# A two-layer diffusion trunk on one core: in the second mixer, VectorE gates the convolved x tile before the next weight split instead of after it

## What is computed

```
def ssd_mixer(h, hc, w_in, conv_w, conv_b, dt_bias, a_log, d_skip, gn_w, w_out):
    ...
    def project(t):
        z, xbc, dt = jnp.split(t @ w_in, [SSD_D_INNER, 2 * SSD_D_INNER + 2 * G * N], axis=-1)
        xbc = jax.nn.silu(conv_centred(xbc, conv_w, conv_b)).astype(jnp.float32)
        xs, Bm, Cm = jnp.split(xbc, [SSD_D_INNER, SSD_D_INNER + G * N], axis=-1)
    ...
    for d, rev in ((0, False), (1, True)):
        yc_d, hc_d = ssd_chunk_scan(f(xc), f(dtc[:, :, d]), A[d], f(Bc), f(Cc), h0)
        yl_d, _ = ssd_chunk_scan(f(xl), f(dtl[:, :, d]), A[d], f(Bl), f(Cl), hc_d)
    ...
    return out(yl, zl), out(yc, zc)      # gate by silu(z), RMS norm, @ w_out
```

## Time and profile before

| what | value |
|---|---|
| median of 3 runs | 2239.76 us (2238.99 to 2245.53) |
| profiled execution, its own time | 2234.72 us |
| span of the profile | 2233.1 us |
| granted TensorE clock, mean | 0.973 of full speed |
| TensorE busy | 2069.7 us (93%) |
| VectorE busy | 1445.1 us (65%) |
| ScalarE busy | 876.2 us (39%) |
| GpSimd busy | 741.8 us (33%) |

### The profile page before, as it was taken

The page is one execution under the profiler, slowest core; times in us unless marked ns, Lnnn a source line. Parts: engine busy times, 40 slices in busy tenths (PEclk is TensorE's granted clock), DMA queues, the critical chain, the costliest instruction groups (busy, mean ns, idle before and its releaser), DMA issues.

```text
span 2233.1 us, 30641 instructions
## 1 busy us (share of the span) xinstructions
PE 2069.7 (93%) x10464; PEld 1686.2 (76%) x10464; DVE 1445.1 (65%) x1832; ACT 876.2 (39%) x1163; POOL 741.8 (33%) x668
## 2 busy tenths in 40 slices
PE   3579999999999999979997999999999999999997
PEld 1157787778777787858885788888888888887776
DVE  1067677767777667662228787778777777778354
ACT  2054444444444444542225333333333333335433
POOL 0066565555556565620110122122222222122001
PEclk8889999999999999989998999999999999999999
DMA  8866665656655666525443545455455546445553
GB/s 356 334 174 170 165 171 160 173 162 170 166 155 154 165 171 163 144 56 119 117 126 88 151 109 145 134 144 135 124 137 141 140 104 155 127 119 181 210 198 139
DMA packets 406312, 349.11 MB, mean 156 GB/s; under 512 B 12320, under 2 KB 361088, under 8 KB 403072
## 3 DMA queue, kind: packets, MB, share of 16 engines
q1 hardware_dynamic: 380592, 267.66, 42.0%
q0 software_dynamic: 20400, 74.46, 12.4%
q10 hardware_dynamic: 5280, 6.47, 0.9%
HBM read 344.21 MB, written 4.33 MB: 156 GB/s over the span
## 4 chain that ended last, share of the span: by engine, by line
PE 35%; issue 20%; DMA 15%; DVE 13%; POOL 8%; ACT 8%; DVEq 1%; POOLq 1%; SPq 0%; ACTq 0%
PE bank L328 8%; PE bank L332 8%; PE bank L330 8%; DMA arena<-in_ssd_ada_w_dram 8%; DMA arena<-in_na_ada_w_dram 6%; POOL acc L557 4%; DVE arena L1291 3%; ACT arena L760 3%; DVE arena L1126 2%; PE bank L1759 2%; PE bank L1760 2%; PE bank L1761 2%; ACT w_hi L310 2%; POOL acc L551 2%; DVE w_lo L314 2%
## 5 line engine op out<-in xcount | busy, mean ns | idle before, releaser
L328 PE MATMUL bank<-act_hi,w_hi 128*128 128x512 f32 (+1 forms) x2576 | 962.2, 374 | 47.2 <-DVE w_lo L314 24.2
L332 PE MATMUL bank<-act_hi,w_lo 128*128 128x512 f32 (+1 forms) x2576 | 940.4, 365 | 0.0
L330 PE MATMUL bank<-act_lo,w_hi 128*128 128x512 f32 (+1 forms) x2576 | 939.9, 365 | 0.0
L314 DVE TENSOR_TENSOR w_lo<-arena,w_hi 128x2048 fp32r<-128x2048 f32 x193 | 470.6, 2438 | 229.5 <-ACT w_hi L310 153.0
L328 PEld LDWEIGHTS bank<-act_hi,w_hi 128*128 128x128 f32 x2576 | 489.5, 190 | 134.4 <-DVE w_lo L314 30.1
L332 PEld LDWEIGHTS bank<-act_hi,w_lo 128*128 128x128 f32 x2576 | 489.2, 190 | 78.5
L330 PEld LDWEIGHTS bank<-act_lo,w_hi 128*128 128x128 f32 x2576 | 490.0, 190 | 74.1
L557 POOL TENSOR_TENSOR acc<-acc,arena 128x512 f32<-128x512 f32 x224 | 315.9, 1410 | 143.6 <-ACT arena L760 134.4
L1126 DVE SCALAR_TENSOR_TENSOR arena<-arena,cond_c 128x512 f32<-128x512 f32 x240 | 262.4, 1094 | 106.2 <-DMA arena<-in_ssd_ada_w_dram 74.7
L760 ACT ACTIVATE arena<-arena,cond_c 128x512 f32<-128x512 f32 x256 | 171.3, 718 | 381.8 <-POOL acc L557 174.7
L310 ACT ACTIVATE w_hi<-arena 128x2048 fp32r<-128x2048 f32 x145 | 276.6, 1907 | 107.4 <-PE bank L1761 79.7
(11 more groups left out here) (208 smaller groups left out, 1845.4 us busy)
## 6 DMA issues: line engine op xcount, KB each, us to landing
arena<-in_ssd_w_in_dram SPq DMA_DIRECT2D x81, 1024.0 KB, 6.0
arena<-in_na_w_in_dram SPq DMA_DIRECT2D x64, 1024.0 KB, 6.9
arena<-in_ssd_ada_w_dram POOLq DMA_DIRECT2D x96, 512.0 KB, 4.1
arena<-in_na_ada_w_dram SPq DMA_DIRECT2D x16, 2048.0 KB, 9.4
arena<-in_ssd_w_out_dram SPq DMA_DIRECT2D x32, 1024.0 KB, 5.0
arena<-in_na_ada_w_dram POOLq DMA_DIRECT2D x32, 512.0 KB, 4.1
arena<-in_na_w_out_dram SPq DMA_DIRECT2D x16, 1024.0 KB, 6.5
arena<-cs_scr SPq DMA_DIRECT2D x64, 256.0 KB, 5.3
```

The source lines that it names most:

```text
L314: nc.vector.tensor_tensor(w_lo[:, n0 % 2, :], raw[slot], w_hi[:, n0 % 2, :].bitcast(F32), ALU.subtract).then_inc(s_lo, 1)
L328: nc.tensor.matmul(bank[b][:, 0:cols], w_hi[:, b, w], act_hi3[:, k, 0:cols], start=(k == 0), stop=False)
L330: nc.tensor.matmul(bank[b][:, 0:cols], w_hi[:, b, w], act_lo3[:, k, 0:cols], start=False, stop=False)
L332: mm = nc.tensor.matmul(bank[b][:, 0:cols], w_lo[:, b, w], act_hi3[:, k, 0:cols], start=False, stop=(k == KT - 1))
```

## The change

`conv` ran `nxt()`, the next weight split, between the convolution and the gate for all six convolutions of a group. Now it does so for B and C alone (`idx` 0 and 1); for the four x tiles the gate comes first and `nxt()` behind it.

```
--- before
+++ after
@@ -1293,11 +1293,14 @@
                 m.then_inc(s_u, 1)
-                nxt()
+                if idx < 2:
+                    nxt()
                 dve.wait_ge(s_uth, t6.at(idx + 1))
                 guard()
                 nc.vector.scalar_tensor_tensor(dst, u_th[:, 0:segs, :], 1.0, u, ALU.add, ALU.mult)\
                   .then_inc(s_conv, 1)
+                if idx >= 2:
+                    nxt()
```

## The result

The changed kernel takes 2248.91 us (median of 6 runs, 2246.51 to 2250.65) against 2241.28 us of the kernel before in the same series (6 runs, 2238.99 to 2245.53): the ratio is 1.0031, 95% interval [1.0018, 1.0044], 7.6 us slower. The profiled execution took 2248.51 us, span 2246.9.

What follows compares the result with a forecast made beforehand. The prediction took TensorE to set the pace, busy 100.1 of 101.7 us a loop pass. Groups 1 to 6 gave 5.6 us, group 7 1.5, group 0 0.5: + 7.6 on 2239.8, so 2247.4 us, range 2242 to 2253.5.

Steps and rivals of the forecast that it cites:

- The split's chain: In the loop, wherever TensorE waited for the gate, the next projection starts 3.64 us after the convolution, not 3.25: + 0.39 us.
- Pair 1 costs nothing: Behind the second x tile of a group, the projection starts without needing VectorE; slack of 0.64 us covers the delay.
- Pair 2, 0.39: Behind the third x tile, the projection moves from 3.24 to 3.64 us after the convolution; + 0.40, taken as 0.39.
- Pair 3, 0.16: Behind the fourth x tile, + 0.23 us for the later projection, less 0.07 from GpSimd's third product coming after VectorE's first instruction.
- The rival in which GpSimd keeps its turn: GpSimd's third product still precedes VectorE's first instruction, lengthening the convolution: about 1.8 us a group, + 13 in all; chance 0.14.
- Group 0, + 0.46: In the first loop group TensorE covers pairs 0 and 1; pairs 2 and 3 cost 0.23 us each.
- The last group, + 1.5: Group 7: 0.39 + 0.39 + 0.71 us; before the output projection VectorE's full 0.78 counts, less 0.07.
- I take nothing: Raw-buffer loads go out 1.38 us later, but their buffer is read some 20 us on; no cost was counted.
- a wait of ScalarE for weights from memory: Named sign of error: ScalarE or TensorE waiting for weight loads from memory; no size was given.
- The sum: Whole kernel: 5.6 us for groups 1 to 6, 1.5 for group 7, 0.5 for group 0; together + 7.6.
- the main case: The split's chain with the order on GpSimd's ports flipped: + 7.6 us, own range + 5 to + 10; chance 0.73.
- GpSimd's ports: In pair 3's convolution, whichever of VectorE and GpSimd starts first holds the shared ports; the flipped order wins 0.21 us, 0.07 counted.

## Why the prediction was right, and where its terms were off

It forecast + 7.6 us, and the medians differ by 7.6. The mechanism was right; that the number agrees to the tenth is luck, since the sum missed some terms and the interval of the difference is about 3 us to each side.

- **What bounds the loop.** Right: TensorE's matmuls are busy for 100.0 us of a pass before and 100.3 after, and most of what the pass grew is time in which TensorE stood still.
- **The split's chain, + 0.39 where TensorE waited for the gate.** Right to 0.01 us with the change in pair 0 alone; gate at C + 0.70, projection at C + 3.64. The kernel without the tanh's wait, and the two kernels with a longer tanh, show that VectorE's loss of cover is the cause.
- **Pair 1 costs nothing.** Right: 0.00 alone.
- **Pair 2, 0.39.** 0.43 alone and 0.47 with the rest, from the convolution's start to the next one's; its convolution, which meets GpSimd, is 0.05 longer (5.50 against 5.45), which the sum did not have.
- **Pair 3, 0.16.** 0.21 (21.47 against 21.26, mean of groups 2 to 6). The order at GpSimd's products flipped as said, product 0.33 behind and first instruction 0.66, and 0.07 was won as said. What was too low is the distance, C + 3.72 for 3.64. The rival in which GpSimd keeps its turn is out. TensorE's wait there was forecast below pair 2's 0.7 and is 0.82 us. In group 1 nothing was won and 0.4 lost: before, its first instruction was not held up (0.55 us), now it takes 0.92. The sum took all six passes alike.
- **Group 0, + 0.46.** Measured + 0.46, to the last digit by luck: the same group differs by 0.3 us between traces in which the change should cost nothing there.
- **The last group, + 1.5.** Measured + 2.57: the failed step is "I take nothing" for the loads. The load itself stayed covered in the loop, but the first output weight tile stands behind the broadcast loads that wait for the decay arguments, was issued 0.4 us later and took 0.6 longer, and a high part and the tanh stand behind it on ScalarE. The cover was next to nothing, about 0.02 us. The prediction had named a wait of ScalarE for weights from memory as a sign of being wrong; this one grew from 3.74 to 4.74 us. With the load issued early the last group costs + 1.60, close to the + 1.5. That TensorE waits for line 1481 there is the prediction's reading of the times; its row names no instruction.
- **The sum.** The pass was forecast at 102.6 and is 102.73; the trace has 9.7 us for the change where 7.6 were said. The median difference of 7.6 has an interval of about 3 us to each side, so it does not decide between them. The range given for the main case, + 5 to + 10, does not follow from its own terms, which add up to about + 6 and + 11.
- **GpSimd's ports.** The prediction let VectorE's first instruction wait out the product that was ahead of it. The traces show this for all convolution instructions (last section). The Trainium skill, "SBUF — State Buffer", section "SBUF: two separate sides", has whichever of the two starts first hold the shared ports for its whole instruction while the other fully blocks. The traces agree with the full block. With "starts first" they agree only up to a tenth of a microsecond of the starts on record: a product that started 0.12 us behind VectorE's instruction still went ahead of it.

## What to carry to other kernels

An instruction that stands between a producer and the wait for a slower engine's answer is cover; before it is moved behind the wait, ask whether the consumer waits for that one next. The wait that a view names (17.4 us for the gate) is only worth what is left when the next condition is counted. Where the covering instruction is longer than the wait and itself on the chain, cut it: the first part covers and the second follows, as the two cuts did here, 1.13 us a pass below the kernel before. And look at the last pass by itself: what stands behind the loop can have less cover than the same instruction inside it.

## What the runs showed of the hardware

- A stop of TensorE of 1.78 us for a split, after 0.4 us of transposes, was followed in five of seven loop groups by about 3.8 us at a granted clock of 0.57, which cost 1.6 us (pair 0 of the changed kernel with the longer tanh). The changed kernel itself, with a stop of 1.60 us at the same place, showed full clock each time. The stop's length alone does not decide: the same 1.78 us in the two other groups, and 1.77 us behind pair 3 of the last group, were followed by full clock. What else does, no run here shows.
- VectorE's wait shows as 0.70 us idle, though the split would have started 0.08 before the convolution's reported end: two instructions of one engine overlap by about 0.08, and a wait between them loses this too.
- VectorE and GpSimd took turns, each for a whole instruction. In all thirteen traces every convolution instruction of 512 columns that took longer than it does alone ended a fixed time behind the end of a GpSimd instruction: the first (line 1288, 0.55 us alone) 0.28 us behind, in 324 of 324 cases, the four others (line 1291, 0.75 us alone) 0.55 us behind, in 741 of 741. The product whose turn came next ended 0.60 or 1.15 us behind VectorE's instruction. The rows after pair 3 above show it: the second product ends at 1514.39 and the first instruction at 1514.67; the third product ends at 1515.82, and the second convolution instruction takes 1.56 us, to 1516.37:

```profile
1514.81 1.56 DVE L1291 SCALAR_TENSOR_TENSOR arena<-arena,convc 128x512 f32<-128x512 f32 x1
```

- Which product the first instruction waited for: the third when it started ahead or up to 0.12 us behind (1.70 us, the row below, from the kernel before with the longer tanh), the second when the third was to start 0.14 us behind or later. At 0.33 to 0.37 behind, the first instruction took 0.65 to 0.69 us.

```profile
1334.41 1.70 DVE L1291 TENSOR_SCALAR arena<-arena,convc 128x512 f32<-128x512 f32 x1 [3.12 <-ACT arena L860]
...
1334.53 1.29 POOL L640 TENSOR_TENSOR arena<-arena 128x512 f32<-128x512 f32 x1
```
